# One level of Strassen's scheme for 8 of the 11 groups of the gate and up projections of a four-layer trunk

## The reference, cut to what matters

```python
def swiglu_ffn(h, w_gate, w_up, w_down):
    return (jax.nn.silu(h @ w_gate) * (h @ w_up)) @ w_down
```

## Time and profile before

| | us |
|---|---|
| median of three runs | 2778.58 |
| profiled execution, its own time | 2777.52 |
| span of that execution, first to last instruction | 2775.8 |
| TensorE busy | 2763.9 (100%) |
| VectorE busy | 1354.9 (49%) |
| ScalarE busy | 1021.0 (37%) |
| GpSimd busy | 610.4 (22%) |

### The profile page before, as it was taken

How to read it: one execution, slowest core, us unless ns; L and a number is a source line. 1 busy time by engine, 2 the same in 40 slices (tenths; PEclk the granted TensorE clock), 3 DMA queues, 4 the chain that set the end, 5 groups by cost and what they waited for, 6 DMA issues and landing times. The chain is left out here.

```text
span 2775.8 us, 37592 instructions
## 1 busy us (share of the span) xinstructions
PE 2763.9 (100%) x14344; PEld 2322.1 (84%) x14344; DVE 1354.9 (49%) x1889; ACT 1021.0 (37%) x1637; POOL 610.4 (22%) x506
## 2 busy tenths in 40 slices
PE   9999999999999999999999999999999999999999
PEld 7888888888888888888888888888888888888888
DVE  4464543345668663333655555543335464543333
ACT  5332432225257552322443443432224332432222
POOL 0021322203113442220321121322202022322211
PEclk9999999999999999999999999999999999999999
DMA  5323233333620123333322223233333333233331
GB/s 170 91 84 92 81 102 99 96 100 108 169 62 2 42 81 106 91 104 95 107 88 81 77 83 99 82 101 97 93 97 111 88 91 87 73 109 100 91 97 65
DMA packets 448359, 256.08 MB, mean 92 GB/s; under 512 B 9728, under 2 KB 431984, under 8 KB 448112
## 3 DMA queue, kind: packets, MB, share of 16 engines
q1 hardware_dynamic: 446944, 251.69, 31.3%
q10 hardware_dynamic: 1296, 2.75, 0.3%
HBM read 248.11 MB, written 2.10 MB: 90 GB/s over the span
## 5 line engine op out<-in xcount | busy, mean ns | idle before, releaser
L1808 DVE SCALAR_TENSOR_TENSOR w_lo<-w_raw,w_hi 128x1024 fp32r<-128x1024 f32 x461 | 635.4, 1380 | 848.3 <-ACT w_hi L1350 847.5
L601 PE MATMUL acc<-a_hi,w_hi 128*128 128x512 f32 (+1 forms) x2136 | 835.8, 391 | 0.3 <-DVE g_lo L2245 0.3
L603 PE MATMUL acc<-a_hi,w_lo 128*128 128x512 f32 (+1 forms) x2136 | 829.0, 388 | 0.0
L602 PE MATMUL acc<-a_lo,w_hi 128*128 128x512 f32 x1944 | 756.6, 389 | 0.0
L1350 ACT ACTIVATE w_hi<-w_raw 128x1024 fp32r<-128x1024 f32 x460 | 483.3, 1051 | 524.2 <-PE acc L603 468.7
L603 PEld LDWEIGHTS acc<-a_hi,w_lo 128*128 128x128 f32 x2136 | 401.1, 188 | 82.9
L601 PEld LDWEIGHTS acc<-a_hi,w_hi 128*128 128x128 f32 x2136 | 401.3, 188 | 82.3 <-DVE g_lo L2245 1.2
L602 PEld LDWEIGHTS acc<-a_lo,w_hi 128*128 128x128 f32 x1944 | 365.2, 188 | 74.5 <-issue 1.0
L603 PE MATMUL acc<-hid_hi,w_lo 128*128 128x512 f32 (+1 forms) x704 | 264.5, 376 | 0.0
L602 PE MATMUL acc<-hid_lo,w_hi 128*128 128x512 f32 (+1 forms) x704 | 264.5, 376 | 0.0
L601 PE MATMUL acc<-hid_hi,w_hi 128*128 128x512 f32 (+1 forms) x704 | 264.5, 376 | 0.0
(11 more groups left out here) (387 smaller groups left out, 3713.9 us busy)
## 6 DMA issues: line engine op xcount, KB each, us to landing
w_raw<-ffn_w_gate SPq DMA_DIRECT2D x88, 512.0 KB, 3.8
w_raw<-ffn_w_up SPq DMA_DIRECT2D x88, 512.0 KB, 3.8
w_raw<-gm_w_in SPq DMA_DIRECT2D x64, 512.0 KB, 4.1
w_raw<-ffn_w_down SPq DMA_DIRECT2D x64, 512.0 KB, 3.8
w_raw<-ret_w_in SPq DMA_DIRECT2D x48, 512.0 KB, 3.8
w_raw<-gm_w_out SPq DMA_DIRECT2D x32, 512.0 KB, 3.8
w_raw<-ffn_w_down SPq DMA_DIRECT2D x32, 384.0 KB, 3.4
w_raw<-nsa_w_in SPq DMA_DIRECT2D x21, 512.0 KB, 4.2
```

The costliest lines, as they stand in the source:

```text
L601: pe.matmul(o_bank, lhs_hi, rhs_hi, start=start, stop=False)
L602: pe.matmul(o_bank, lhs_hi, rhs_lo, start=False, stop=False)
L603: return pe.matmul(o_bank, lhs_lo, rhs_hi, start=False, stop=stop)
L1808: dve.scalar_tensor_tensor(w_lo[:, slot, :, :], w_raw[:, slot, :, :], 1.0, w_hi[:, slot, :, :].bitcast(f32), ALU.mult, ALU.subtract).then_ ...
```

## The change

Eight of the eleven groups of each layer (2 to 9, `SEVEN_FROM, SEVEN_TO = 2, 10`) are computed by one level of Strassen's scheme. A pair of units, now two gate tiles or two up tiles, makes a product of 256 features, 1024 inputs and 512 tokens. It is cut in two in each of the three, and the eight block products of 128 x 512 x 256 become seven, each of 12 matmuls of 256 columns.

- GpSimd makes four sums of weight blocks for each pair (`weight_sums`, 128x512 each), in place buffers of which there is one set: each waits until TensorE has used the one before it (`s_used`). At the layer's start it also makes four sums of token blocks (`token_sums`, 128x1024 each) from a scaled copy `a_full` of the stream, which ScalarE writes.
- ScalarE and VectorE split these sums into high and low parts (`sums_high`, `sums_low`, `tokens_high`, `tokens_low`). The second unit of a pair needs only its lower half split (`unit_rows`).
- Pair 0 accumulates in the banks `tr` and `st`, pair 1 in `acc`. VectorE joins the seven products (`join`: four tensor_tensor from PSUM, each waiting for the one before; the first also for a copy by ScalarE of one product), GpSimd or VectorE multiplies by `R`, ScalarE applies silu to two tiles at once.
- The gated tiles are stored in float32 (`hid_full`). Their split into `hid_hi` and `hid_lo` is left to group 10, with ten low parts on VectorE and twelve on GpSimd.
- Groups 0, 1 and 10 stay as they were but for the order gate, gate, up, up.
- The loads of groups 3 and later wait for the weight sums of the group before (`s_sum`) in place of `lo_done`.
- Some semaphores of the gMLP mixer are merged into fewer, with the same order of work.

The core of the diff (indentation shortened; in it, the second `seven` and the ones after it are of ScalarE, VectorE and GpSimd):

```diff
+SEVEN_FROM, SEVEN_TO = 2, 10
...
+def seven_banks(pair):
+  low = (tr[:, :, :] if pair == 0 else acc[:, 1:3, :]).rearrange("p a n -> p (a n)")
+  return low, st[:, 0, :] if pair == 0 else acc[:, 0, :], st[:, 1, 0:HALF] if pair == 0 else acc[:, 3, 0:HALF]
...
+def unit_rows(i, j):
+  return slice(DT // 2, DT) if (j == 0 and is_seven(i)) or (j == 2 and is_seven(i + 1)) else slice(0, DT)
...
+    def up_group(i):
+      for j in range(4):
+        slot = (L["n_up"] + j) % SLOTS
+        src = cols((ffn_w_gate if j < 2 else ffn_w_up)[l], 0, D_MODEL, i * (2 * P) + (j % 2) * P)
+        if isinstance(i, int) and i <= SEVEN_FROM:
+          load(i * 4 + (L["n_up"] + j), slot, src, DT)
+          continue
+        sp.wait_ge(s_sum, i * 8 + (68 * l - 16 + 4 * (j // 2)))
+        sp.dma_start(w_raw[:, slot, :, :], src.rearrange("(k p) m -> p k m", p=P)).then_inc(loaded[slot], 16)
+    loop(sp, 11, up_group, SEVEN_FROM + 1)
...
+    def block_product(out_half, lhs_hi, lhs_lo, rhs_hi, rhs_lo):
+      for k in range(DT // 2):
+        last = product(out_half, lhs_hi[:, k, :], lhs_lo[:, k, :], rhs_hi[:, k, :], rhs_lo[:, k, :], k == 0, k == DT // 2 - 1)
+      return last
+    def seven(i):
+      for pair in range(2):
+        slot0, slot1 = (n0 + 2 * pair) % SLOTS, (n0 + 2 * pair + 1) % SLOTS
+        low, x, p1 = seven_banks(pair)
+        top, bottom = slice(0, DT // 2), slice(DT // 2, DT)
...
+        for r, (k, out_half, t) in enumerate([(1, low[:, 2 * HALF:3 * HALF], 0), (3, low[:, 3 * HALF:4 * HALF], 2),
+                           (2, x[:, second], 1), (4, low[:, HALF:2 * HALF], None)]):
+          pe.wait_ge(s_lo, sums_base(L, i, pair) + (8 if begun else r + 1))
+          rhs_hi = a_hi[:, bottom, second] if t is None else t_hi[:, t, :, :]
+          rhs_lo = a_lo[:, bottom, second] if t is None else t_lo[:, t, :, :]
+          block_product(out_half, left[k][0], left[k][1], rhs_hi, rhs_lo).then_inc(s_used, 1)
+        pe.wait_ge(lo_done, i * 4 + (n0 + 2 * pair + 1))
+        block_product(p1, w_hi[:, slot0, top, :], w_lo[:, slot0, top, :], a_hi[:, top, first], a_lo[:, top, first]).then_inc(s_used, 1)
+        block_product(x[:, first], w_hi[:, slot0, bottom, :], w_lo[:, slot0, bottom, :], a_hi[:, bottom, first], a_lo[:, bottom, first]).then_inc(unit_done, 1)
+        pe.wait_ge(lo_done, i * 4 + (n0 + 2 * pair + 2))
+        block_product(low[:, 0:HALF], w_hi[:, slot1, bottom, :], w_lo[:, slot1, bottom, :], t_hi[:, 3, :, :], t_lo[:, 3, :, :]).then_inc(unit_done, 1)
+    entry(L["b_mid"])
+    plain(1)
+    seven(SEVEN_FROM)
+    with pe.Fori(0, SEVEN_TO - SEVEN_FROM - 1) as r:
+      seven(r + (SEVEN_FROM + 1))
+    plain(SEVEN_TO)
...
+    def tokens_high():
+      for t in range(4):
+        act.wait_ge(s_sum, 68 * L["layer"] + 4 + t + 1)
+        act.activation(t_hi[:, t, :, :], t_full[:, t, :, :], ACT.Copy).then_inc(s_hi, 1)
+    def hid_high(t0, t1):
+      for t in range(t0, t1):
+        act.wait_ge(hid_mul, q0 + (t // 2 * 2 + 2 if t < 2 * SEVEN_TO else t + 1))
+        act.activation(hid_hi[:, t, :], hid_full[:, t, :], ACT.Copy).then_inc(hid_hi_done, 1)
...
+    def plain(i):
+      if i == 1:
+        for t in range(DT):
+          last = act.activation(a_full[:, t, :], h[:, t, :], ACT.Copy, scale=gain[:, gain_of(L["b_mid"]), t:t + 1])
+        last.then_inc(p1_out, 1)
       for j in range(4):
         if not begun_split(i, j):
-          ahead(L["n_up"], i, 4, j)
-    loop(act, 11, swiglu, 1)
+          ahead(n0, i, 4, j, unit_rows(i, j))
+        if i == SEVEN_TO:
+          act.wait_ge(unit_done, n0 + 4 * SEVEN_TO)
+          hid_high(*[(0, 10), (10, 15), (15, 2 * SEVEN_TO), (0, 0)][j])
+        if j < 2:
+          silu_plain(i, j)
+        if i == 1 and j == 2:
+          sums_high(SEVEN_FROM, 0)
+          tokens_high()
+      if i == SEVEN_TO:
+        hid_high(2 * SEVEN_TO, FT)
+    def seven(i):
+      for pair in range(2):
+        ahead(n0, i, 4, 2 * pair, unit_rows(i, 2 * pair))
+        if pair == 0:
+          sums_high(i, 1)
+        elif not (isinstance(i, int) and i == SEVEN_TO - 1):
+          sums_high(i + 1, 0)
+        if pair:
+          act.wait_ge(m_step, i * 7 + (56 * L["layer"] - 14 + 4))
+          act.activation(work[:, 0:2, :], work[:, 0:2, :], ACT.Silu).then_inc(silu_done, 2)
+        act.wait_ge(s_used, used_base(L, i, pair) + 5)
+        act.activation(sq[:, pair, 0:HALF], seven_banks(pair)[2], ACT.Copy).then_inc(p1_out, 1)
+        ahead(n0, i, 4, 2 * pair + 1, unit_rows(i, 2 * pair + 1))
...
+    def sums_low(i, pair):
+      for r, k in enumerate((0, 2, 1, 3)):
+        if k < 2:
+          dve.wait_ge(s_sum, sums_base(L, i, pair) + (3 if k == 0 else 4))
+        dve.wait_ge(s_hi, sums_base(L, i, pair) + (r + 1))
+        dve.scalar_tensor_tensor(s_lo_of[k][:, :, :], s_full_of[k][:, :, :], 1.0, s_hi_of[k][:, :, :].bitcast(f32),
+                    ALU.mult, ALU.subtract).then_inc(s_lo, 1)
+    def tokens_low():
+      for t in range(4):
+        if t < 2:
+          dve.wait_ge(s_sum, 68 * L["layer"] + 4 + (2 if t == 0 else 4))
+        dve.wait_ge(s_hi, 68 * L["layer"] + 4 + t + 1)
+        dve.scalar_tensor_tensor(t_lo[:, t, :, :], t_full[:, t, :, :], 1.0, t_hi[:, t, :, :].bitcast(f32),
+                    ALU.mult, ALU.subtract).then_inc(s_lo, 1)
+    def plain(i):
       for j in range(4):
         if not begun_split(i, j):
-          ahead(L["n_up"], i, 4, j)
-
-        if j % 2 == 0:
-          wait(dve, hid_lo_done, i * 2 + (L["q_up"] + j // 2 - 1))
-        leave(i * 4 + (L["n_up"] + j), work[:, j, :], (L["o_up"] + j) % BANKS, R[:, :])
-    loop(dve, 11, swiglu, 1)
+          ahead(n0, i, 4, j, unit_rows(i, j))
+        if i == SEVEN_TO and j == 0:
+          join(SEVEN_TO - 1, 1)
+          for t in range(FT // 2 - 1):
+            dve.wait_ge(hid_hi_done, q0 + t + 1)
+            dve.scalar_tensor_tensor(hid_lo[:, t, :], hid_full[:, t, :], 1.0, hid_hi[:, t, :].bitcast(f32),
+                        ALU.mult, ALU.subtract).then_inc(hid_lo_done, 1)
+        if i == 1 and j == 2:
+          sums_low(SEVEN_FROM, 0)
+          tokens_low()
+        wait(dve, hid_mul, q0 + (2 * SEVEN_TO if i == SEVEN_TO else 2 * i - 1 + j % 2))
+        dve.wait_ge(unit_done, i * 4 + n0 + j + 1)
+        dve.tensor_tensor(work[:, j, :], up_bank(L, i, j), R[:, :], ALU.mult).then_inc(acc_free, 1)
+    def join(i, pair):
+      low, x, _ = seven_banks(pair)
+      both = work[:, 2 * pair:2 * pair + 2, :]
+      steps = 56 * L["layer"] - 14 + 4 * pair
+      dve.wait_ge(hid_mul, i * 2 + q0)
+      dve.wait_ge(p1_out, i * 2 + (17 * L["layer"] + 1 - 4 + pair + 1))
+      dve.wait_ge(unit_done, i * 4 + (n0 + 2 * pair + 1))
+      dve.tensor_tensor(both[:, :, 0:HALF], by_side(x), sq[:, pair, 0:HALF].unsqueeze(1).broadcast_to([P, 2, HALF]), ALU.add).then_inc(m_step, 1)
+      dve.wait_ge(m_step, i * 7 + (steps + 1))
+      dve.tensor_tensor(both[:, :, HALF:SEQ], by_side(low[:, 2 * HALF:4 * HALF]),
+               work[:, 2 * pair + 1, 0:HALF].unsqueeze(1).broadcast_to([P, 2, HALF]), ALU.add).then_inc(m_step, 1)
+      dve.wait_ge(unit_done, i * 4 + (n0 + 2 * pair + 2))
+      dve.wait_ge(m_step, i * 7 + (steps + 2))
+      dve.tensor_tensor(work[:, 2 * pair + 1, 0:HALF], low[:, 0:HALF], work[:, 2 * pair + 1, HALF:SEQ], ALU.add).then_inc(m_step, 1)
+      dve.wait_ge(m_step, i * 7 + (steps + 3))
+      dve.tensor_tensor(both[:, :, HALF:SEQ], by_side(low[:, HALF:3 * HALF]), both[:, :, HALF:SEQ], ALU.add).then_inc(acc_free, 2)
+      if pair == 0:
+        dve.wait_ge(acc_free, i * 4 + (o0 + 2))
+        dve.tensor_tensor(both, both, R[:, :].unsqueeze(1).broadcast_to([P, 2, SEQ]), ALU.mult).then_inc(m_step, 1)
+    def seven(i):
+      for pair in range(2):
+        ahead(n0, i, 4, 2 * pair, unit_rows(i, 2 * pair))
+        if pair:
+          join(i, 0)
+        elif not (isinstance(i, int) and i == SEVEN_FROM):
+          join(i - 1, 1)
+        if pair == 0:
+          sums_low(i, 1)
+        elif not (isinstance(i, int) and i == SEVEN_TO - 1):
+          sums_low(i + 1, 0)
+        ahead(n0, i, 4, 2 * pair + 1, unit_rows(i, 2 * pair + 1))
...
+    def weight_sums(i, pair):
+      slot0, slot1 = (n0 + 2 * pair) % SLOTS, (n0 + 2 * pair + 1) % SLOTS
+      pool.wait_ge(loaded[slot0], i * 16 + 16 * ((n0 + 2 * pair) // SLOTS + 1))
+      pool.wait_ge(loaded[slot1], i * 16 + 16 * ((n0 + 2 * pair + 1) // SLOTS + 1))
+      a11, a12 = w_raw[:, slot0, 0:DT // 2, :], w_raw[:, slot0, DT // 2:DT, :]
+      a21, a22 = w_raw[:, slot1, 0:DT // 2, :], w_raw[:, slot1, DT // 2:DT, :]
+      full = [t[:, :, :] for t in s_full_of]
+      used, done = used_base(L, i, pair) - 5, sums_base(L, i, pair)
+      wait(pool, s_used, used + 1)
+      pool.tensor_tensor(full[0], a21, a22, ALU.add).then_inc(s_sum, 1)
+      wait(pool, s_used, used + 2)
+      pool.tensor_tensor(full[2], a11, a21, ALU.subtract).then_inc(s_sum, 1)
+      wait(pool, s_used, used + 3)
+      pool.wait_ge(s_sum, done + 1)
```

(53 more changed lines are left out.)

140 lines of the change are left out of this document (93 added, 47 removed).

## The result

The changed kernel takes 2913.49 us (median of 4 runs, 2908.61 to 2917.35) against 2778.73 for the one before: 1.0483 times as long, 95% interval 1.0465 to 1.0502. I had forecast slower, 2884, and the range to 2915 holds the time, close to its upper end. The profiled execution has a span of 2906.9 us against 2775.8: 131.1 more, 32.8 a layer where I had 26.3.

The account below looks back on a forecast made before the run. TensorE bounds the kernel before; in the change, VectorE and GpSimd excluding each other outweighs its saving. Per layer 15.3 + 7 + 4 = 26.3, four layers 105, on 2777.5 gives 2882.7, plus 1.1: 2884 us; range 2745 to 2915.

Parts of the forecast that it names:

- TensorE's saving, 1.6 us a group: Eight groups of each layer: TensorE's matmuls go from 21.76 to 20.16 us a group, 51.2 us over 32 groups.
- VectorE and GpSimd exclude each other: Eight groups: two-SBUF-input VectorE instructions and GpSimd's wait for each other's end; per 512 columns GpSimd holds 1.11 us, VectorE 0.53.
- The product by `R` in the sum: VectorE's product by `R`, one a group: counted as 1.07 us of the exclusion, with no row showing it beside GpSimd.
- The sum 21.8: Time a group in which either engine holds the port: 13.3 us by GpSimd plus 8.5 by VectorE.
- The walk: A group followed instruction by instruction: 21.8 plus 1.4 free port plus 1.2 handing over, 24.4 us; also walked start and end.
- The eight groups, 189.4: Groups 2 to 9 of a layer: 20.3 + 6 x 24.4 + 22.7 = 189.4 us against 174.1, 15.3 more.
- The start, 7: Before group 2: TensorE waits for weight and token sums and their splits; 7 us a layer taken, walk 7.9, ends 2.5 and 9.
- The end, 4: Down projection: TensorE waits for late hidden low parts; 4 us a layer taken, walk 6, ends 0 and 7.
- the clock falls: Rival: TensorE's idle time at the start lowers its clock, some 10 us in all, 2894; chance inside the main forecast's 0.64.
- TensorE the bound: Rival: VectorE and GpSimd run side by side, eight groups cost 161.3, start 2.5, 41 us less in all, 2738; chance 0.19.
- the deciding hold of 0.88 for 512 columns: Sign for TensorE as bound: GpSimd holds 10.6 us a group in place of 13.3, 0.88 for 512 columns.
- Packed tight: Rival: port used without gaps, eight groups 172.8, start 6, end 1.5, 6.2 us more a layer, 2803; chance 0.12.

Follow-up runs that it names:

- the experiment: Changed kernel with, for the start, token sums and splits 128 columns wide: 2865.84 us; for the end, GpSimd's late hidden low parts 64 columns wide: 2876.48 us.
- 2908.96: Changed kernel plus idle matmuls keeping TensorE busy, 68 before group 2 and 14 before each later group, nothing left out: 2908.96 us.
- the last experiment: Changed kernel without VectorE's two-SBUF-input instructions in the eight groups, with narrow token sums and narrow late low parts: 2728.47 us, 0.9823 of the kernel before.

## Why the forecast was right, and where it was short

*TensorE's saving, 1.6 us a group:* right within 2 us over the whole run (49.5 between the medians, 50.9 between the traces), once nothing else is in the way.

*VectorE and GpSimd exclude each other:* right. With VectorE's low parts of sums kept in place and in length but reading one input, the eight groups fall from 188.4 to 170.0; with all its two-input instructions so changed they take 164.1, with GpSimd's work whole. The hold of a sum, that is its end after VectorE's, is 1.13 to 1.16 where I had 1.11, that of a low part 0.55 where I had 0.53.

*The product by `R` in the sum:* it excludes GpSimd (2.07 at 370.47), but was worth 0.35 us a group and not 1.07. The Trainium skill (SBUF — State Buffer, section Who interferes with whom) counts it among those that contend, and the 2.07 agrees. The sum 21.8 by itself is no time: with the sums' low parts out it falls to 17.5, below TensorE's 20.16, and the later groups still took 21.65. The walk added 2.6 us of free time and handing over to this sum and came to 24.4; no run prices these terms one by one, so how well the total fits is in part luck.

*The eight groups, 189.4:* measured 188.4, on average over the layers 189.1. Periods of 24.7 and 24.1 against 24.4, the first 21.5 against 20.3, the last 21.7 against 22.7. The parts fit less well than the whole: TensorE's waits per group are 2.2 to 2.35 before pair 0 where I had 2.5, in pair 1 1.1 where I had 1.7, and none at all in the groups of 24.1, in which 1.6 us of slow pace take that place.

*The start, 7:* measured 8.6 of waiting, and 10.9 between the traces of the experiment, with what follows from it. I had walked 7.9 and chosen 7; nothing in the rows spoke for less than the walk. The four token sums took 11.8 where I had 9.6.

*The end, 4:* this is the term that was furthest off. Measured 8.3, and 8.2 between the traces of the experiment. I had GpSimd's late low parts at 1.30 each; ten took 14.98:

```profile
563.07 14.98 POOL L2842 TENSOR_TENSOR hid_lo<-hid_full,hid_hi 128x512 fp32r<-128x512 f32 x10 [7.64 <-ACT hid_hi L1902]
578.01 1.27 POOL L2828 TENSOR_TENSOR hid_full<-work 128x512 f32<-128x512 f32 x1
...
580.09 1.26 POOL L2842 TENSOR_TENSOR hid_lo<-hid_full,hid_hi 128x512 fp32r<-128x512 f32 x1 [0.80 <-ACT hid_hi L1902]
```

They start at 563.07, behind high parts of ScalarE that come after group 10's first silu, and after them each of the two last tiles costs product, high part and low part in a row, 3.3 us, where I had counted 2.6 of GpSimd's own time. TensorE waits 2.34 and 2.15 for these two. The walk had 6 here too, which is what the gaps of the waits came to (6.2), and I took 4. The other 2.1 of the 8.3 is the slow clock, for which I had nothing in this place.

*The sum:* on average over the four layers the start is +1.8, the end +4.5, the eight -0.3, and 0.5 isn't placed: 6.5 a layer, 26 us. The median lies 4.9 above the profiled execution's own time, 1.1 in the forecast. That is the 29.5.

*The rival "the clock falls", some 10 us:* the clock did fall. In the eight groups it made 34 us of slow matmuls, and its price there is 10 us at most (2908.96 against 2913.49, with intervals that overlap). In the down projection, which I hadn't named, it is 2.1 to 2.4 us a layer, some 9 us in all, and lies on the path by the traces. So the size I had guessed was about right, by luck: the place was another. *TensorE the bound* is what the last experiment shows at 2728, but only with the other work gone; the deciding hold of 0.88 for 512 columns was never near: the 139 sums show 1.13 to 1.16. *Packed tight*, 2803, didn't happen. That the single set of sum buffers is why isn't shown: the first sum's idle time is put down to TensorE's product for 139 us in all, but it is 138.5 too where the exclusion is gone and the groups take 20.16. No run has a second set.

## What to carry to other kernels

Before moving work to an idle GpSimd, list what VectorE does beside it and how it reads: with two inputs in SBUF, or in a quick one-input form, it works only while GpSimd's reading instructions don't, and they only while it doesn't. Add their times in the new stage, but then walk the order, for the sum is neither a floor nor a forecast of one edit's worth. Price the entry and the exit of a new scheme as carefully as its steady part: here they are 17 of 31 us a layer; where a walk has been made, do not shade its figure down. Price a slow clock by what follows it: in the eight groups TensorE would have waited anyway and the clock cost next to nothing, behind the last wait of the down projection TensorE never waited again, and there the slow pace is simply lost.

## What I had not expected of the hardware

A tensor_scalar of 512 columns, one input, takes 0.36 us alone and 1.74 beside GpSimd; a tensor_reduce of the same columns takes 0.68 in both. As stand-ins for the low parts, the slower instruction gave a kernel 41 us faster than the quick one.

In the eight groups 34 us of slow matmuls were worth 10 us at most, and groups with them came even 0.6 us sooner (24.10 against 24.74).

An instruction of GpSimd that reads only 32 columns can wait for VectorE as a wide one does: the short sums between fills take up to 1.28 us, with a mean of 0.457 in one form, against 0.25 where VectorE was elsewhere:

```profile
L2790 POOL TENSOR_TENSOR s_full<-w_raw 128x32 f32<-128x32 f32 x128 | 58.5, 457 | 164.5 <-PE tr L652 143.8 <-PE acc L652 20.1
```
